# Eight of 19 modulation chunks multiplied and summed over their k-tiles by VectorE, each chunk's sums added into the PSUM bank by TensorE with a column of ones

## The reference, cut to what matters

```
# in meaning:
mods = silu(c) @ mod_w[layer] + mod_b[layer]     # c: 2 vectors of 2048; mod_w[layer]: 2048 x 6144
shift, scale, gate = split(mods, 3)
```

## Time and profile before

| | |
|---|---|
| median of 3 runs | 2440.16 us (2439.88 to 2441.19) |
| profiled execution, its own time | 2443.28 us |
| its span in the trace | 2441.2 us |
| PE / DVE / ACT busy | 2421.8 / 1488.0 / 1189.6 us |
| plain-fp32 modulation matmuls (L901) | from 173.5 to 1007.5 us of the span |

### The profile page before, as it was taken

One profiled execution on the slowest core, in us unless ns is written; L12 is line 12 of the kernel. 1 busy time (PEld: TensorE's weight loads), 2 busy tenths in 40 slices (PEclk: granted clock), 3 DMA queues, 4 the chain that ended last, 5 costly groups with the idle time before them and its releaser, 6 DMA issues.

```text
span 2441.2 us, 31070 instructions
## 1 busy us (share of the span) xinstructions
PE 2421.8 (99%) x11777; PEld 1921.6 (79%) x11777; DVE 1488.0 (61%) x2043; ACT 1189.6 (49%) x1758; POOL 127.6 (5%) x84
## 2 busy tenths in 40 slices
PE   9999999999999999999999999999999999999999
PEld 7887777787777777888888888888887887878877
DVE  6644445564545555667676767875556476664865
ACT  6644344653544444556656666424425344253462
POOL 0000000000000000013211111001300000000000
PEclk9999999999999999999999999999999999999999
DMA  8578887737787777565333333555435444354444
GB/s 286 172 213 268 252 270 254 242 118 257 243 272 232 254 242 246 186 242 128 104 95 98 95 97 92 183 187 165 130 111 157 129 121 146 114 153 130 129 128 148
DMA packets 285440, 432.54 MB, mean 177 GB/s; under 512 B 20855, under 2 KB 100109, under 8 KB 284301
## 3 DMA queue, kind: packets, MB, share of 16 engines
q1 hardware_dynamic: 284140, 422.56, 55.6%
q10 hardware_dynamic: 1184, 8.41, 0.9%
HBM read 428.79 MB, written 2.12 MB: 177 GB/s over the span
## 4 chain that ended last, share of the span: by engine, by line
PE 94%; DVE 2%; ACT 2%; DMA 1%; issue 1%; POOL 0%; SPq 0%; ACTq 0%; DVEq 0%
PE ps L826 67%; PE ps L1238 13%; PE ps L901 3%; PE ps L1219 2%; PE ps L1014 1%; PE ps L877 1%; PE ps L979 1%; PE ps L1346 1%; PE ps L1364 1%; PE ps L1191 1%; PE ps L999 1%; DMA ring<-in_att_w_out 1%; ACT ring_hi L1483 1%; DMA ring<-in_att_w_in 0%; PE ps L1355 0%
## 5 line engine op out<-in xcount | busy, mean ns | idle before, releaser
L2018 DVE TENSOR_TENSOR ring_lo<-ring,ring_hi 128x1024 fp32r<-128x1024 f32 (+2 forms) x576 | 694.1, 1215 | 625.1 <-ACT ring_hi L1483 620.9
L1483 ACT CAST ring_hi<-ring 128x1024 fp32r<-128x1024 f32 (+2 forms) x598 | 619.6, 1040 | 893.6 <-PE ps L826 499.6
L826 PE MATMUL ps<-ring_hi,act_hi 128*128 128x512 f32 (+2 forms) x1272 | 505.9, 398 | 2.3 <-ACT proj L1562 1.2
L826 PE MATMUL ps<-ring_hi,act_lo 128*128 128x512 f32 (+2 forms) x1272 | 490.8, 386 | 0.0
L826 PE MATMUL ps<-ring_lo,act_hi 128*128 128x512 f32 (+2 forms) x1272 | 489.6, 385 | 0.0
L826 PE MATMUL ps<-ring_hi,features_hi 128*128 128x512 f32 x1152 | 457.5, 397 | 1.0 <-issue 0.8
L826 PE MATMUL ps<-ring_hi,features_lo 128*128 128x512 f32 x1152 | 449.2, 390 | 0.0
L826 PE MATMUL ps<-ring_lo,features_hi 128*128 128x512 f32 x1152 | 448.6, 389 | 0.0
L826 PEld LDWEIGHTS ps<-ring_hi,act_hi 128*128 128x128 f32 x1272 | 239.1, 188 | 71.7 <-issue 20.9
L826 PEld LDWEIGHTS ps<-ring_hi,act_lo 128*128 128x128 f32 x1272 | 238.8, 188 | 49.4
L826 PEld LDWEIGHTS ps<-ring_lo,act_hi 128*128 128x128 f32 x1272 | 239.4, 188 | 43.5
(11 more groups left out here) (291 smaller groups left out, 2459.0 us busy)
## 6 DMA issues: line engine op xcount, KB each, us to landing
ring<-in_mod_w SPq DMA_DIRECT2D x192, 512.0 KB, 4.7
ring<-in_att_w_in SPq DMA_DIRECT2D x128, 512.0 KB, 3.8
ring<-in_ev_w_in SPq DMA_DIRECT2D x104, 512.0 KB, 4.7
ring<-in_od_w_in SPq DMA_DIRECT2D x96, 512.0 KB, 5.0
ring<-in_lru_w_in SPq DMA_DIRECT2D x64, 512.0 KB, 4.1
ring<-in_ev_w_out SPq DMA_DIRECT2D x40, 512.0 KB, 4.2
ring<-in_lru_w_out SPq DMA_DIRECT2D x40, 512.0 KB, 4.2
ring<-in_od_w_out SPq DMA_DIRECT2D x36, 512.0 KB, 4.8
```

The lines of the kernel that those rows point to most:

```text
L826: mm = pe.matmul(PS[:, bank, 0:n], a, w[:, k - k0, :], start=(k == k_first and j == 0), stop=(k == k_last and j == 2))
L1483: act.copy(high(U, n), raw(U, n)).then_inc(s_hi, 1)
L2018: dve.tensor_tensor(out=low(U, n), in0=raw(U, n), in1=high(U, n).bitcast(F32), op=ALU.subtract).then_inc(s_lo, 1)
```

## The change

Of the 19 chunks, eight (`SUMMED`: 2, 3, 6, 7, 10, 11, 14, 15) are no longer multiplied by TensorE. Their 64 units are named "sum_mod" in the ring. VectorE takes each of them from its raw slot with four instructions (`summed_mod`: two k-tiles x two condition vectors; the first two of a chunk only multiply). The accumulators are two pieces of 128x512 in a part of the projection rows that is free at that time (`summed_rows`). When a chunk's 32 instructions are done, TensorE sums the accumulators over their 128 partitions: four matmuls of 256 columns with `OZ`, a column of ones among zeros, into the chunk's place of the bank (in `fill_mod`, ahead of the first "mod" pair behind the chunk's last sum_mod unit). TensorE waits there for the chunk's 32nd step; VectorE begins the next summed chunk only when TensorE has passed that place. SP waits for VectorE's steps before it loads over a sum_mod unit.

So 32 of the 76 pairs leave TensorE, 8 x 4 matmuls of 256 columns come to it, and 256 instructions of 128x512 come to VectorE. The ring keeps its 450 units ahead of the odd layer's output product, and the order of split units; the plan tables spread sum_mod units singly behind split units where pairs stood before.

```diff
 N_MOD = 19
+SUMMED = (2, 3, 6, 7, 10, 11, 14, 15)
...
-def with_mod(units, pairs, before_head=False):
+def with_mod(units, pairs, before_head=False, summed=()):
...
         out += units[k:k + 1]
+        if k in summed:
+            out.append(("sum_mod", next(SUMMED_UNITS)))
...
-EV_TURNS = lay_turns(0, [(MEM_EV, 0, (3, 4, 4, 3), (1, 2, 1, 1)), (MEM_EV, 1, (3, 4, 4, 3), (1, 2, 1, 1)), (MOBA, 0, (3, 4, 4, 3), (1, 2, 1, 1)),
...
+EV_TURNS = lay_turns(0, [(MEM_EV, 0, (3, 4, 4, 3), (1, 0, 1, 0), ((0,), (0, 2), (0, 2), (0,))), (MEM_EV, 1, (3, 4, 4, 3), (0, 1, 0, 1), ((0,), (0, 2), (0,), (0,))),
...
 def used_by(U):
-    return 2 if U + 1 < len(RING) and RING[U + 1][0] in ("gate_mod", "host_mod") else 1
+    return 2 if U + 1 < len(RING) and RING[U + 1][0] in ("sum_mod", "gate_mod", "host_mod") else 1
...
+                    if RING[back][0] == "sum_mod":
+                        m, j = divmod(RING[back][1], 8)
+                        sp.wait_ge(s_am, 32 * SUMMED.index(m) + 4 * (j + 1))
...
+                if u in SUM_ADDED:
+                    n = SUM_ADDED.index(u)
+                    at_row = 2 * (SUMMED[n] - ROUND_AT[r])
+                    pe.wait_ge(s_am, 32 * (n + 1))
+                    for w in range(2):
+                        for half in range(2):
+                            g, cols = 64 * w + 32 * half, slice(half * CHUNK // 2, (half + 1) * CHUNK // 2)
+                            pe.matmul(PS[g:g + MOD_COLS, MB, cols], OZ[:, MOD_COLS - 1 - at_row - w:2 * MOD_COLS - 1 - at_row - w],
+                                      summed_rows(n)[w][:, cols], start=False, stop=False)
...
+            def summed_mod(u):
+
+                m, j = divmod(u, 8)
+                n = SUMMED.index(m)
+                U = POS["sum_mod", u]
+                if n and j == 0:
+                    dve.wait_ge(s_wused, POS["mod", SUM_ADDED[n - 1]] + 1)
+                dve.wait_ge(s_w[U % SLOTS], landed(U))
+                for k in range(2 * j, 2 * j + 2):
+                    for w in range(2):
+                        rows, by, acc = raw(U)[:, k % 2 * CHUNK:(k % 2 + 1) * CHUNK], CS[:, 2 * k + w:2 * k + w + 1], summed_rows(n)[w]
+                        if k == 0:
+                            ins = dve.tensor_scalar(acc, rows, by, None, ALU.mult)
+                        else:
+                            dve.wait_ge(s_am, 32 * n + 2 * k + w - 1)
+                            ins = dve.scalar_tensor_tensor(out=acc, in0=rows, scalar=by, in1=acc, op0=ALU.mult, op1=ALU.add)
+                        ins.then_inc(s_am, 1)
...
                     lo_to(split_behind(U - 1))
+                    if unit[0] == "sum_mod":
+                        summed_mod(unit[1])
```

More of the change, by code:

```diff
@@ L194, in round_chunks @@
 def round_chunks(r):
-    return range(ROUND_AT[r], ROUND_AT[r + 1])
+    return [m for m in range(ROUND_AT[r], ROUND_AT[r + 1]) if m not in SUMMED]
 def round_end(r):
@@ L209, in __init__ @@
         self.even = heads in (MEM_EV, MOBA, MLA)
-MOD_UNITS = iter(range(8 * N_MOD))
-def with_mod(units, pairs, before_head=False):
+MOD_UNITS = iter([8 * m + j for m in range(N_MOD) if m not in SUMMED for j in range(8)])
+SUMMED_UNITS = iter([8 * m + j for m in SUMMED for j in range(8)])
+def with_mod(units, pairs, before_head=False, summed=()):
     out, n = [], len(units)
@@ L231, in lay_turns @@
     turns, at = [], 0
-    for j, (heads, i, counts, pairs) in enumerate(plan):
+    for j, (heads, i, counts, pairs, summed) in enumerate(plan):
         gaps = []
-        for count, p in zip(counts, pairs):
-            gaps.append(with_mod(units[at:at + count], p, True))
+        for count, p, behind in zip(counts, pairs, summed):
+            gaps.append(with_mod(units[at:at + count], p, True, behind))
             at += count
@@ L262 @@
-OD_TURNS = lay_turns(10, [(SWA[j], i, (1, 3, 2, 1), (0, 1, 1, i % 2)) for j in range(2) for i in range(4)]
-                     + [(DIL, 0, (1, 3, 1, 1), (0, 1, 1, 0)), (DIL, 1, (1, 2, 1, 1), (0, 1, 1, 0)), (DIL, 2, (1, 2, 1, 1), (0, 1, 1, 0)),
-                        (MEM_OD, 0, (1, 1, 1, 1), (0, 1, 1, 0)), (MEM_OD, 1, (1, 2, 1, 0), (0, 0, 0, 0))],
+OUT_MID = with_mod(OUT_C1[4:] + [("ev_out", 10 * c + u) for c in range(2) for u in range(4)] + [("ev_out", u) for u in range(20, 32)], 5,
+                   summed=(0, 2, 4, 6, 8, 10, 12, 13, 16, 18, 20))
@@ new lines @@
+OUT_LAST = [("ev_out", 38), ("ev_out", 39)]
+OD_FIRST = with_mod(chunk_units("od_b", [0])[2:], 0, summed=(1, 4))
+OD_SECOND = with_mod(chunk_units("od_b", [2]), 1, summed=(1, 4, 6))
+OD_THIRD = with_mod(chunk_units("od_b", [8]), 2)
+OD_TURNS = lay_turns(10, [(SWA[j], i, (1, 3, 2, 1), (0, 0, 1, 0), ((), (0,), (0,), ())) for j in range(2) for i in range(4)]
+                     + [(DIL, 0, (1, 3, 1, 1), (0, 2, 1, 0), NONE), (DIL, 1, (1, 2, 1, 1), (0, 2, 1, 0), NONE), (DIL, 2, (1, 2, 1, 1), (0, 2, 1, 0), NONE),
+                        (MEM_OD, 0, (1, 1, 1, 1), (0, 1, 1, 1), NONE), (MEM_OD, 1, (1, 2, 1, 0), (0, 0, 0, 0), NONE)],
@@ L265 @@
                      chunk_units("od_b", OD_FILL) + chunk_units("od_c", [0]))
-assert next(MOD_UNITS, None) is None
+assert next(MOD_UNITS, None) is None and next(SUMMED_UNITS, None) is None
 RING = []
@@ L398 @@
 ROWS_BY = {next(s for s in SPLIT_UNITS if s > POS["mod", round_end(r)]): r for r in range(N_ROUND)}
-SUMS_BY = {max(s for s in SPLIT_UNITS if s < POS["mod", round_end(r) + 1]): r for r in range(N_ROUND - 1)}
+SUMS_BY = {max(s for s in SPLIT_UNITS if s < POS["mod", 8 * ROUND_AT[r + 1]]): r for r in range(N_ROUND - 1)}
 SUMS_BY[POS[OD_TURNS[-1].gaps[1][1]]] = N_ROUND - 1
 assert len(ROWS_BY) == len(SUMS_BY) == N_ROUND and all(r <= s for r, s in zip(sorted(ROWS_BY), sorted(SUMS_BY)))
+SUM_ADDED = []
+for _m in SUMMED:
+    _r = next(r for r in range(N_ROUND) if ROUND_AT[r] <= _m < ROUND_AT[r + 1])
+    _u = next(u for name, u in RING[POS["sum_mod", 8 * _m + 7]:] if name == "mod")
+    assert _u % 2 == 0 and 8 * ROUND_AT[_r] < _u <= round_end(_r)
+    SUM_ADDED.append(_u)
+assert sorted(set(SUM_ADDED)) == SUM_ADDED
+assert all(POS["mod", u] < POS["sum_mod", 8 * m] for u, m in zip(SUM_ADDED, SUMMED[1:]))
 def evicted(stage, c):
@@ L581, in build, with summed_rows @@
         CZ = SC[:, 0:(KT + 1) * MOD_COLS - 2]
+        OZ = SC[:, 140:139 + 2 * MOD_COLS]
+        def summed_rows(n):
+            H, c = (HE, 8) if SUM_ADDED[n] <= round_end(ROUNDS_BEFORE_MLA - 1) else (HO, 7)
+            return [H[:, w, c * CHUNK:(c + 1) * CHUNK] for w in range(2)]
         SQX, SQL, SQC, SQG = (SC[:, j:j + 8].rearrange("p (t c) -> p t c", t=TT) for j in (72, 56, 64, 80))
```

28 lines of the change are left out of this document (15 added, 13 removed).

## The result

| kernel | median | runs | ratio to before |
|---|---|---|---|
| before | 2440.51 us | 5 (2439.88 to 2441.32) | |
| changed | 2466.42 us | 5 (2463.25 to 2469.41) | 1.0108, 95% interval 1.0096 to 1.0119 |

The forecast was 2418.0 us with a range of 2407 to 2431. The change costs 26 us where it was to save 22. The rest of this part reads the profiled execution of the changed kernel (2467.58 us, span 2465.5 against 2441.2).

A forecast was written before the change was run, and what follows sets the result against it. TensorE was taken as the bound (busy 2421.8 of 2441.2 us). Terms -37.1 + 4.4 + 8.6 + 2 = -22.1 us brought the median of 2440.16 to 2418.0 us, with 2407 to 2431 as the range for 8 in 10.

The forecast's parts named there:

- What TensorE loses and gets: On TensorE, 32 pairs go (37.1 us) and eight products with ones come (4.4 us): 32.7 us saved without any wait.
- What VectorE gets: On VectorE, eight summed chunks of 21.5 us add 172 us; at 75% busy it is not the bound on average.
- The wait at A: TensorE, ahead of the products with ones, awaits a chunk's last sum: 1.6 us at three places, 1.9 at two, 8.6 in all.
- The slots: Ring slots of summed units are freed about 3.5 us later; covered by 3 us, so 2 us of waits (0 to 10).
- The softmax moves covered: A head's softmax moves back by up to one sum, covered by a gap of three or four units of TensorE.
- VectorE's own new wait costs nothing: VectorE begins a summed chunk only when TensorE has passed A; it gets there behind TensorE anyway, so nothing is added.
- the loop through the ring: Late sum, late load, late low half, later next sum; decides beyond 6.6 us behind TensorE; 2461 us, 8%.
- rival 2: Half given back: 3 to 4 us waits at A, late low halves in dense stretches; 2428 us (2424 to 2435), 17%.
- The pair's line: Sign in the new profile: the line of the pair matmuls has 352 records instead of 608.
- The last pair: Sign on TensorE: the end of the last pair comes at about 985 us instead of 1007.5.
- The 6.0 us of waits for low halves: Sign: TensorE's idle time ahead of split units, 6 us before, stays under 10; over 20 means rival 2 or 3.
- The waits of casts for landings: Companion sign: these waits grow if TensorE's idle time for low halves is over 20 us; longest before 7.2 us.

The follow-up runs named there:

- best1: lead4_shift with, besides, VectorE's copy of the rope keys three ring places earlier; 2415.7 us, ratio 0.9890 to the kernel before.
- hold2: Kernel before, with SyncE loading the slot of the first unit of each of the first 64 pairs only after TensorE used two more places; 2453.3 us, ratio 1.0044.
- hold3: As hold2 on the kernel before, but held for three more places of TensorE instead of two; 2500.1 us, ratio 1.0235.
- lead4: Changed kernel with VectorE's sums four ring places earlier (the fifth chunk's first sum stays); 2430.9 us, ratio 0.9956 to the kernel before.
- lead2: Changed kernel with VectorE's sums two ring places earlier; 2437.5 us, ratio 0.9989 to the kernel before.
- lead4_shift: lead4 with one pair moved from the third dilated turn to the next turn; 2423.4 us, ratio 0.9923 to the kernel before.
- places: Changed kernel, sums unmoved, with best1's two edits (shifted pair, earlier copy of the rope keys); 2458.5 us, ratio 1.0072 to the kernel before.

## Why the prediction was wrong, step by step

**What TensorE loses and gets: right.** The forecast was -32.7 us. best1, which has the same TensorE instructions at full clock, is busy for 2421.8 - 2390.1 = 31.7 us less. The product with ones was taken at 0.55 us. In the changed kernel's timeline of TensorE it starts 0.43 us ahead of the pair behind it, somewhat below the lower bound of 0.49, half a pair:

```profile
242.88 0.62 PE L931 MATMUL ps<-proj,scalars 128*8 128x256 f32 x8 [2.45 <-DVE proj L2177]
243.31 1.04 PE L936 MATMUL ps<-ring,scalars 128*8 128x512 f32 x8
```

**What VectorE gets: right, a little high.** It was 172 us; the pages differ by 1648.4 - 1488.0 = 160.4, since a sum and the low half beside it overlap by some 0.1 us at each end. Four instructions take 2.73 us at 745 ns each, as in the earlier trace rows, so here too the next one starts ahead of the end of the one before. The prediction read the Trainium skill too strictly here: the page "VectorE: DVE Perf Modes", section "The DRAIN you can't avoid", adds to its drain: "A next op that is not held starts earlier", that is, one that need not wait for those ahead of it to finish. These rows agree with that.

**The wait at A: right in its places and its sum, wrong in shape.** It was 8.6 us at five places; the row says 9.2 us, 5 times, and at the same five. But they are 2.4 (turn 0), 1.3 (turn 5), 4.0 (OUT_MID), 1.2 (turn 13) and 0.2 us (turn 17) in place of 1.6 and 1.9, so that the sum came out is part luck. In best1 the line of ones waits for no VectorE step. The wait belonged to the place of the sums, and not to the product.

**The slots: this step failed.** The prediction had each sum 3.5 us late, the landing 3.5 + 4.8 = 8.3 us after TensorE's passing, 3 us of room left, and a price of 2 us (0 to 10). The mean was nearly right: 4.3 and 8.7 us. Wrong was what followed from it. The room was worked out for one slot on its own, from a mean, with SyncE, ScalarE and VectorE free when the slot came free. But all three work in order, and a slot that is late holds back the loads, casts and sums of the places behind it, which are late then on their part. hold2 and hold3 measure it: from 7.7 to 10.8 us of mean landing the loss goes from 11 to 58 us, where the prediction's room would have been 3.7 and 0.6 us. The 35 us between the changed kernel and lead4 hold this step, with the half clock behind its gaps, and the 9.2 us at A, which are gone in lead4 too. Without A some 26 us are left, against the 2 that were written down. What of them belongs to the copy of the rope keys, which the next step is about, can't be told apart: its wait fell from 10.5 to 4.6 us in lead4.

**"The softmax moves covered", "VectorE's own new wait costs nothing": what else stands behind a sum was not gone through.** The softmax was right: no transpose of probabilities waits in the list above, and the values (L1051) wait 0.2 us as before. (With the sums moved, as in lead2, it isn't always so.) But the copy of the rope keys, a single copy behind EV_SECOND's last sum, held TensorE for 10.5 us, and the rows of the fifth round for 4.1: the new plan leaves one split unit between that round's end and its sums, where there were four. best1 prices the first at 7.7 us and lead4_shift the second at 7.6, each with its clock, even when the ring doesn't run short. The prediction looked at the places around A alone.

**The clock: not in the prediction.** Every term took work at full clock. 13.5 us were lost at the lower level behind the gaps, a third on top of the idle time.

**The whole miss.** The forecast's span was 2441.2 - 22.1 = 2419.1 us, and it came to 2465.5, which is 46.4 more. The work that leaves TensorE was put 1.0 us too high, TensorE's added idle time is 42.5 us where 8.6 + 2 were written down, and 13.5 is the clock: 1.0 + 31.9 + 13.5 = 46.4.

**The rivals.** The third one, "the loop through the ring", gave 2461 us and came nearest (2466.4). It was given 8%, with the argument that the loop gains about 2 us per round, and its point of decision at 6.6 us behind TensorE. It needed less: the mean is 4.3 us, and 9 of 64 sums lie beyond 6.6. The argument against it took three units and a share of a head per round of the loop everywhere. In EV_SECOND and OUT_MID, where a sum stands behind every one or two low halves, that share of a head isn't there. The prediction had named these stretches in rival 2, but priced them at 20 us of waits without the clock.

**The signs.** The pair's line has its 352 records. The last pair began at 1038.0 us and not at about 985; in best1, which hardly waits, it began at 984.2. The 6.0 us of waits for low halves that the sign started from are those of TensorE's weight loads; its matmuls waited for none before. The same row is 11.2 us now, and the one of the matmuls 10.5, at the edge of "under 10": by that sign alone the ring looks nearly sound. The waits of casts for landings, named as the companion sign, tell more; in the list of waits from 173 to 1007 us they grew from 103.9 to

```profile
ACT ring_hi L1520 <- DMA ring<-in_ev_w_in: 139.8, 56, 10.1
```

## What to carry to other kernels

When work moves to another engine and that engine then frees a shared buffer, its place in that engine's queue matters more than its duration: here the same instructions made the kernel 1.1% slower or 0.4% faster, and with two small moves 1.1% faster. Judge the room of a ring by the latest slots and by everything that is issued in order behind them, and not by the mean of one slot; a test that only delays slots measures it within two runs. List all that stands behind the added instructions on their engine up to the next thing that the busiest engine awaits, and allow for the slower clock behind gaps of 2 us and more.

## What the runs showed of the hardware

The granted clock of TensorE fell to half behind six single gaps of 2.5 to 10.5 us in a stretch that is otherwise busy for 95% of the time, and it was at half for 3.2 us of work behind the largest. The length of a gap doesn't decide it alone: in the same trace the clock stayed at 1.00 behind a gap of 2.67 us (at 376.0 us), and in places it fell behind one of 1.61 us (at 767.7). It didn't fall at the largest gap when useless products filled 8.7 us of it. A plain fp32 product of 128 stationary and 512 moving columns takes 0.86 us (27.63 us for 32), against 0.227 us from one product of a split unit to the next (10.91 us for 48); so the three products that the kernel makes in place of one plain one, 0.68 us, are still cheaper.
